# Mixed steps of the scan and the latent attention placed anew, and weight casts and low parts dealt out anew among ScalarE, VectorE and GpSimd

## What is computed

```python
u = rms_norm(h, mix_pre_g[l])
hq, hf, hi, hg, cq, ckv, kpe, gates = jnp.split(u @ w_in[l], splits, axis=-1)
y_a = hgrn2_mixer(hq, hf, hi, hg, lower_bounds[l], hg_norm_g[l]) @ w_hg_o[l]
y_b = mla_mixer(cq, ckv, kpe, q_norm_g[l], w_q_b[l], kv_norm_g[l], w_kv_b[l], cos, sin) @ w_mla_o[l]
gate_a, gate_b = jnp.split(jax.nn.sigmoid(gates + b_gate[l]), 2, axis=-1)
mixed = (gate_a * y_a + gate_b * y_b) @ w_out[l]
```

## Time and profile before

| What | Value |
|---|---|
| Median of 3 runs | 898.12 us (897.7 to 898.27) |
| The profiled execution | 897.94 us, span 896.1 us |
| TensorE matmuls | 884.4 us, 99% of the span |
| VectorE | 667.4 us, 74% |
| ScalarE | 466.3 us, 52% |
| GpSimd | 200.4 us, 22% |
| Granted TensorE clock | 0.999 |

### The profile page before, as it was taken

One profiled execution on the slowest core, in us unless ns is written; L12 is line 12 of the kernel. 1 busy time (PEld: TensorE's weight loads), 2 busy tenths in 40 slices (PEclk: granted clock), 3 DMA queues, 4 the chain that ended last, 5 costly groups with the idle time before them and its releaser, 6 DMA issues.

```text
span 896.1 us, 16529 instructions
## 1 busy us (share of the span) xinstructions
PE 884.4 (99%) x6641; PEld 782.7 (87%) x6641; DVE 667.4 (74%) x1253; ACT 466.3 (52%) x940; POOL 200.4 (22%) x113
## 2 busy tenths in 40 slices
PE   9999999999999999999999999999999999999997
PEld 8879999989999798888888899977888888888886
DVE  7745987586447877786666767768888788788885
ACT  7444336665344774444444657866553545543443
POOL 4123421531132120553214522230001111210100
PEclk9999999999999999999999999999999999999999
DMA  8356453153424746555564374215354465465441
GB/s 331 114 184 234 140 174 112 48 212 142 142 96 145 278 163 236 188 196 187 187 219 169 124 247 165 97 48 211 142 222 161 182 213 204 152 230 188 174 156 48
DMA packets 23180, 153.66 MB, mean 171 GB/s; under 512 B 2864, under 2 KB 3248, under 8 KB 5568
## 3 DMA queue, kind: packets, MB, share of 16 engines
q1 hardware_dynamic: 22384, 150.44, 46.8%
q0 software_dynamic: 576, 2.10, 0.6%
q10 hardware_dynamic: 144, 0.07, 0.0%
HBM read 151.28 MB, written 1.05 MB: 170 GB/s over the span
## 4 chain that ended last, share of the span: by engine, by line
PE 96%; DVE 2%; ACT 1%; issue 1%; DVEq 0%; ACTq 0%
PE pb L528 94%; PE pb L531 2%; ACT FA L534 1%; DVE FA L537 0%; DVE wl L537 0%; ACT R L534 0%; DVE X L543 0%; DVE wh L552 0%; DVE FA L546 0%; ACT wh L534 0%; DVE FA L540 0%; DVE st L540 0%; DVE st L555 0%; DVEq L585 0%; DVE FA L543 0%
## 5 line engine op out<-in xcount | busy, mean ns | idle before, releaser
L528 PE MATMUL pb<-R,wh 128*128 128x256 f32 (+2 forms) x2224 | 545.5, 325 | 3.3 <-DVE R L543 2.0
L528 PE MATMUL pb<-R,wl 128*128 128x256 f32 (+1 forms) x1512 | 420.0, 281 | 0.0
L528 PEld LDWEIGHTS pb<-R,wh 128*128 128x128 f32 x2224 | 369.5, 188 | 43.3 <-ACT R L534 3.4
L537 DVE TENSOR_TENSOR wl<-raw,wh 128x1024 fp32r<-128x1024 f32 (+1 forms) x207 | 273.3, 1344 | 76.6 <-ACT wh L534 74.8
L537 POOL TENSOR_TENSOR wl<-raw,wh 128x1024 fp32r<-128x1024 f32 (+1 forms) x71 | 173.4, 2445 | 581.5 <-ACT wh L534 427.4
L528 PEld LDWEIGHTS pb<-R,wl 128*128 128x128 f32 x1512 | 283.4, 188 | 1.7
L534 ACT ACTIVATE wh<-raw 128x1024 fp32r<-128x1024 f32 (+1 forms) x223 | 226.1, 1044 | 52.0 <-PE pb L528 36.9
L528 PE MATMUL pb<-wh,R 128*128 128x512 f32 (+1 forms) x704 | 227.1, 389 | 0.1
L528 PEld LDWEIGHTS pb<-wh,R 128*128 128x128 f32 x704 | 131.7, 188 | 31.1 <-issue 1.7
L534 ACT ACTIVATE FA<-pb 128x256 f32<-128x256 f32 (+7 forms) x240 | 93.2, 411 | 118.4 <-PE pb L528 103.2
L528 PE MATMUL pb<-wl,R 128*128 128x512 f32 (+1 forms) x352 | 135.5, 385 | 0.0
(11 more groups left out here) (127 smaller groups left out, 434.6 us busy)
## 6 DMA issues: line engine op xcount, KB each, us to landing
raw<-in_w SPq DMA_DIRECT2D x137, 1024.0 KB, 4.8
X<-in_x SPq DMA_DIRECT2D x2, 512.0 KB, 4.1
raw<-in_w SPq DMA_DIRECT2D x2, 512.0 KB, 6.8
post<-in_ffn_post SPq DMA_DIRECT2D x2, 512.0 KB, 4.3
post<-in_w POOLq DMA_DIRECT2D x2, 512.0 KB, 4.9
FA<-in_w POOLq DMA_DIRECT2D x2, 512.0 KB, 8.0
out<-X SPq DMA_DIRECT2D x4, 256.0 KB, 2.0
cst<-in_cst SPq DMA_DIRECT2D x1, 822.5 KB, 12.6
```

Source lines behind the costliest of these rows:

```text
L528: return self.real.matmul(*a, **k) if self.real else self
L537: return self.real.tensor_tensor(*a, **k) if self.real else self
```

## The change

Only two strings change, MADE and the entries "scan" and "latent" of MIX (the entry "maps" is broken over its lines at another place and is the same string). The set of steps and of instructions for each step is the same, but for which engine casts and subtracts.

```diff
-MADE = ("dpdpddddddddqdpdpdddpddpvpvdppqpdddppddddpddvqpqpqpdpddddpdddpqddvdpddppddpddpddpddvvdddqdvdddpd"
+MADE = ("dpdpddddddddqdpdpdddpddpvpvdppdpvppqqqppqppdqqdvvpvpqddpdpvvddqpqddpvqqqdpppvppdpddvvdddqdvdddpd"
...
-    "scan": "..abc.aabc..bb.c..ab.bc...a.b.b..cc...bcb.c..a..cc...bc.b.ca.bbcd.c..cbcbad.bd.c.e.b.ecf.ef.f.f.f",
-    "latent": "..a......aaaaaaaa................bc....b.fgc.b..f.c.g..de.b.cf...d.gf.e.hi.dg.h.e.d..ie.h..i.h..i",
+    "scan": "a.ba.ba..cbc.b...bc.ca...b..a.cbb..c.b.bc.c....cbc..d.bcc..cbaa.bc.b..cbcdb.dac..be.c.eeff.ff..."
+            "f",
+    "latent": "a.......aa.a.aaa..a.a............bc..b..gc.f..cb..f..d.e....bgfd..cg..i.h.d.h.fheig.....di.he.e."
+            "i",
```

More of the change, by code:

```diff
@@ L424 @@
 MIX = {
-    "scan": "..abc.aabc..bb.c..ab.bc...a.b.b..cc...bcb.c..a..cc...bc.b.ca.bbcd.c..cbcbad.bd.c.e.b.ecf.ef.f.f.f",
-    "latent": "..a......aaaaaaaa................bc....b.fgc.b..f.c.g..de.b.cf...d.gf.e.hi.dg.h.e.d..ie.h..i.h..i",
+    "scan": "a.ba.ba..cbc.b...bc.ca...b..a.cbb..c.b.bc.c....cbc..d.bcc..cbaa.bc.b..cbcdb.dac..be.c.eeff.ff..."
+            "f",
+    "latent": "a.......aa.a.aaa..a.a............bc..b..gc.f..cb..f..d.e....bgfd..cg..i.h.d.h.fheig.....di.he.e."
+            "i",
     "out1": "............c.caac..aaacabab.bbaaaaaa.baaabbbcbbbbbbbbccc....",
     "ffn1": "..aaaaac..acaba......aaaaaaaa....bbbbccbb......b.bbbb...bbbb............",
-    "maps": "...a.....acbabcbc..cc.bbb.ede.eed.ecag.agcdgcggadc.b.bfcgbefdc.ab.dgfbe.dbhffbbhhhfa.ccccf.igecbeif."
-            "gahf.ddib.b.bbigchijbjj..cbhcibchkhajkhcikkhcjbiijbcijkijkcijg.kjjkk.ggkkij.k.",
+    "maps": "...a.....acbabcbc..cc.bbb.ede.eed.ecag.agcdgcggadc.b.bfcgbefdc.ab.dgfbe.dbhffbbhhhfa.ccccf.igecb"
+            "eif.gahf.ddib.b.bbigchijbjj..cbhcibchkhajkhcikkhcjbiijbcijkijkcijg.kjjkk.ggkkij.k.",
     "out2": "c.caac..aaacabab.bbaaaaaa.baaabbbcbbbbbbbbccc....",
```

## The result

The change makes the kernel slower by 1.3%: 909.44 us median (907.73 to 912.25) against 898.03 on the same chip, ratio 1.0129 [1.0109, 1.0149]. I forecast 900.6 in a range of 896.4 to 903.2: the direction was right, the size was not. The profiled execution has a span of 908.1 us against 896.1, 12.0 us more.

A forecast was written before the change was run, and what follows sets the result against it. TensorE was taken as the bound, with matmuls busy 99% of the span. 897.94 - 0.8 - 0.3 + 3.2 + 0.4 = 900.4 us for the profiled execution, 900.6 for the median, range 896.4 to 903.2.

The forecast's parts named there:

- part 3: Scan: GpSimd low parts hold VectorE's decays, so TensorE waits ahead of levels; +3.2 us (+2.1 to +4.5).
- My walk: Scan from unit 29: queues followed beside TensorE's calendar; decay (1,3) late 2.6 or 0.2 us, level (1,5) waits 1.9.
- Rivals one and two: Scan: rival one has its own line; two keeps only the wait ahead of level (1,5), +1.9, 898.9 us, chance 0.12.
- the pile-up: Scan waits reach 4.5 us and GpSimd goes first at unit 52, +1.6; 903.1 us, chance 0.10.
- rival one: Scan: GpSimd takes kinder turns, decays (1,3) and (1,4) keep their time; 897.0 us, chance 0.30.
- Part 2: Scan and latent stage: the new order may remove old waits of TensorE; -0.3 us (0 to -0.7).
- Part 1: TensorE: runs of fp32 steps between tiles fall from 40 to 32; -0.8 us (-0.4 to -1.4).
- Part 4: Latent stage: unit 52's low part delays the first qpe rotation and the scores; +0.4 us (0 to +1.6).
- Part 5: Units 58 to 78: GpSimd low parts keep pace with TensorE and cost nothing; up to 1 us each without reserve.

The follow-up runs named there:

- e9: The changed kernel with only the letters of units 33 to 41 of MADE as before; 903.27 us, ratio 1.007.
- e12: e11 with only units 33 to 41 dealt as in the change; 906.29 us, ratio 1.010.
- e11: e5 with level (1,0) and its decay moved behind tile hg 4, and levels (1,5) and (0,5) in the other order; 898.18 us, ratio 1.000.
- e1: The kernel before with the new MADE and the old MIX; 903.93 us, ratio 1.0065.
- e4: The changed kernel with MADE for units 71 to 78 as before; 907.39 us, ratio 1.0103.
- e5: The kernel before with the new MIX and one letter of MADE, unit 42 p instead of d; 900.43 us, ratio 1.0026.
- e7: The changed kernel with three dummy matmuls at the start replaced by 99 small ones, 192 more instructions ahead; 914.64 us.
- e8: The kernel before with three dummy matmuls at the start replaced by 99 small ones, 192 more instructions ahead; 904.31 us.
- e2: The kernel before with the new MIX and the old MADE; 905.75 us, ratio 1.0085.
- e3: The changed kernel with MADE for units 30 to 48 as before; 908.09 us, ratio 1.0112.
- e6: e5 with three dummy matmuls at the start replaced by 99 small ones, 192 more instructions ahead; 902.51 us.

## Why the prediction failed, step by step

**The mechanism of part 3 was right and was priced too low.** VectorE and GpSimd in the changed kernel:

```profile
126.61 5.87 DVE L539 TENSOR_TENSOR FA<-FA 128x512 f32<-128x512 f32 x3
...
133.24 2.45 DVE L539 TENSOR_TENSOR post<-post,cst 128x272 f32<-128x272 f32 x1
...
142.14 3.53 DVE L539 TENSOR_TENSOR FA<-FA 128x512 f32<-128x512 f32 x3
...
126.77 2.78 POOL L539 TENSOR_TENSOR wl<-raw,wh 128x1024 fp32r<-128x1024 f32 x1 [2.16 <-DVE wh L554]
129.97 2.37 POOL L539 TENSOR_TENSOR wl<-raw,wh 128x1024 fp32r<-128x1024 f32 x1 [0.41 <-ACT wh L536]
133.01 2.39 POOL L539 TENSOR_TENSOR wl<-raw,wh 128x1024 fp32r<-128x1024 f32 x1 [0.67 <-ACT wh L536]
...
142.13 2.89 POOL L539 TENSOR_TENSOR wl<-raw,wh 128x1024 fp32r<-128x1024 f32 x1 [0.77 <-ACT wh L536]
```

Decay (1,2) took 5.87 us because GpSimd came in twice, low 37 and then low 38 between two products. My walk let each decay be held once at most. It had decay (1,3) late and put the first wait ahead of level (1,4); in fact decay (1,2) is late, ahead of level (1,3): 1.0 us. Low 39 slips in ahead of the sine product of kpe (2.45 us for the 0.44 of the earlier trace rows), as the walk had low 38 do, decay (0,4) takes 3.6 us (from 138.42) beside low 40, where the walk had it ahead of that low part, and decay (1,4) is held by low 41 (142.13), the wait ahead of level (1,5) being 3.7 us where I had 1.9. Together 4.8 us beyond the usual length of the tiles, against 3.2 (2.1 to 4.5). e9 and e12 show that the letters of units 33 to 41 are the cause. That it is their low parts, and not the four casts that came to VectorE with them, is read from these rows, in which a decay of some 1.4 us takes 3.5 to 5.9 beside low parts, and has no run of its own. Rivals one and two are refuted, and the pile-up had the right direction at too low a price (6.1 us at most). Busy time alone would have spoken for rival one: VectorE's own work became less.

**A wait of TensorE also costs clock, a term that the sum lacked.** The windows of the changed kernel behind the wait of 3.7 us:

```profile
145.70:146.80 1.10, 1.08 (x36) 1.08 (x38) 0.00 (x0) 0.00 (x0) 0.00 (x0) 1.00 0.61 89
146.80:147.80 1.00, 1.00 (x28) 1.00 (x24) 0.00 (x0) 0.83 (x2) 0.00 (x0) 0.53 0.84 344
147.80:148.80 1.00, 1.00 (x16) 0.74 (x13) 0.00 (x0) 0.95 (x3) 0.00 (x0) 0.50 1.04 442
148.80:149.80 1.00, 1.00 (x7) 0.91 (x5) 0.32 (x1) 0.95 (x3) 0.00 (x0) 0.50 0.45 180
149.80:150.60 0.80, 0.80 (x8) 0.80 (x6) 0.36 (x1) 0.75 (x3) 0.00 (x0) 0.71 0.00 0
```

The granted clock falls from 1.00 to 0.50 (2.4 to 1.2 GHz) one microsecond after TensorE has resumed, and stays there till about 150.3. The missing share of those windows is 0.47 + 0.50 + 0.50 + 0.29 x 0.8 = 1.7 us. This is busy time, so no view of waits shows it. The four executions of the changed kernel took 907.73, 908.98, 909.9 and 912.25 us at a mean granted clock of 0.999, 0.998, 0.996 and 0.994: the slower, the lower the clock, and 0.005 of 908 us is 4.5, their spread (roughly, since the mean counts the end of the span too, behind TensorE's work). The fastest had the clock of the kernel before and was still 9.7 us slower.

**Part 2 looked for waits that the order removes and not for those that it makes.** The fetch waits cost 2.05 + 1.01 + 0.75 = 3.8 us beyond the usual length of the steps. Nothing in my text allowed for them: the sum has them at 0 without a reason. The trace of before held the warning: four of its instruction packets in the scan begin only 3.0 to 4.0 us before they are needed, at or behind small steps that stand close. I priced level pairs from the earlier trace rows by the 0.10 us that they save and not by their 256 instructions. The queue of instructions was the one view I hadn't read.

**Part 1, fewer changes of kind (-0.8), and the -0.3 of part 2 brought nothing that can be seen.** e11 has them without waits: the stretches between tiles fell from 22 to 19 in the scan and from 18 to 14 in the latent stage, while hq 7 to kn 0 took 91.68 instead of 91.75 us and kn 0 to yb 0 90.33 instead of 90.34. The row behind a small step is longer, as the earlier trace rows have it, but in the one pair that I compared small steps pay as much among themselves. The four matmuls of ck's norm start 0.72 us before the tile behind them in the kernel before, and in e11, with another small step behind, 1.03 us before that:

```profile
148.71 1.08 PE L528 MATMUL pb<-LN,cst 128*128 128x272 f32 x4
149.43 0.60 PE L528 MATMUL pb<-R,wh 128*128 128x256 f32 x2
```

```profile
147.70 1.19 PE L530 MATMUL pb<-LN,cst 128*128 128x272 f32 x4
148.73 0.60 PE L533 MATMUL pb<-cst,FA 128*128 128x128 f32 x4
```

**Part 4 was right, within its bounds.** The low part of unit 52 lies on qpe's rotation: its product takes 1.40 us in the chain above (206.56), 0.44 otherwise, and the first scores start at 208.47, 0.7 us late, where I had 0.4 (0 to 1.6).

**Part 5, nothing from units 58 to 78, was wrong.** Between yb 7 and the first tile behind the projection the changed kernel loses 1.67 us, e1 1.56 and e9 1.58, with the same letters; e4, with those of units 71 to 78 taken back, and e5 lose none. The chain of the changed kernel there:

```profile
301.25 3.02 PE pb L530 x12
...
304.29 2.95 ACT wh L536 x3
...
307.26 2.53 DVE wl L539
...
311.07 0.62 DVE wh L554
```

and of e4_last_deal_back:

```profile
294.99 13.44 PE pb L530 x69
...
308.53 0.70 DVE wh L554
```

In e4 the chain is TensorE's up to the cast that fills a freed buffer, as in the earlier trace rows (299.14). In the changed kernel it leaves TensorE at 304.3: GpSimd's low parts hold five of the eight evacuations of yb on VectorE (3.4 to 3.7 us instead of 1.8; in the kernel before and in e4 two are held), the casts behind them on ScalarE are late, a low part of VectorE takes 2.53 instead of 1.22, and the cast starts at 311.07, not at once behind TensorE. The price of a low part on GpSimd isn't its own 2.4 us against TensorE's 2.8 a unit, but what it holds on VectorE. My test, that VectorE had 0.37 us idle ahead of 299.14, covered only losses before, not new work in the way.

**The sum.** Fetches 3.8, decays 4.8, half clock 1.7, qpe 0.7, boundary 1.7 are 12.7 us for the 12.0 seen. The 0.7 over isn't settled: the terms are read from single steps, to a few tenths each. The terms aren't independent either, as e7 shows: with the fetch waits taken out of the changed kernel, the waits for decays and the half clock behind them grow by as much. The forecast for the profiled execution was 900.4 and it took 909.9, 9.5 us more. Of these the terms that the sum had at nothing are 7.2 (fetches 3.8, clock 1.7, boundary 1.7), part 3 is 1.6 (4.8 for 3.2), part 4 is 0.3 (0.7 for 0.4), and parts 1 and 2, which brought nothing that can be seen, are 1.1. These are 10.2 us, or 9.5 less the 0.7 over. The range failed since its upper end rested on one mechanism, the lock between VectorE and GpSimd.

## What to carry to other kernels

Where TensorE never waits, ask of a reordering what it adds, in the trace's own terms: how many instructions it puts in how few microseconds, how long before its use each packet of the instruction queue comes, and which slab loads lie in front of it. A dealing of work among VectorE and GpSimd is judged by what VectorE holds ready for TensorE while GpSimd runs, not by busy time. A wait of TensorE costs clock behind it as well: waits of 1.7 to 4 us cost 0 to 3.4 us more here. Look at the granted clock behind each. And an order and the deal that goes with it are one change: one letter was worth 5.3 us here.

## What was not expected of the hardware

- TensorE's instructions come in packets of 16 KB, 256 instructions. The 13 long waits of kind issue in the stages that change (three each in the changed kernel, e4 and e8, one each in e2, e3, e5 and e9) all fall on 193 modulo 256 of TensorE's stream and end 2.2 to 2.5 us after the packet began. Packets begin just as a slab load ends: 100.81 and 117.85 in the changed kernel, 97.39 (slab until 97.41) and 106.48 (until 106.48) in e8. The Trainium skill says (DMA: Bandwidth & Descriptors, section Queues, rings and completion order) that a DMA engine takes its queues in turn and drains a whole packet before it switches; the trace agrees insofar as instructions come behind the slab and not within it, but no run here tells apart how many descriptors such a packet holds.
- Clock behind a wait: 3.4 us at 0.50 after a wait of 3.7 us; 6.8 us at 0.50 in e2, from 148.3, within its wait of 4.0 us, to 155.2; in e12 from about 134.1 to 137.6 after one of 2.6 by the list of waits; in e5, after one of only 1.71, from about 103.8 to 107.2, while the changed kernel's 1.88 at the same place had no such stretch. Executions of one kernel differ in this: e5's two slowest (901.89, which is the profiled one, and 901.38 us, median 900.43) have a mean granted clock of 0.998, the eight others 0.999 or 1.000. Why one wait brings the half clock and another doesn't stays open.
- 99 matmuls of 32 weight columns by 16 in place of three wide ones took 1.7 us longer (7.42 for 5.73 in e8), and behind them the clock was at 0.50 for 6.8 us (from 8.9 to 15.7 in e6, from 8.0 to 14.8 in e8), 4.5 to 4.8 us in all.
